# Shared-head queries rotated with their weight alone, the root applied to the row maximum and in the exponential

## The reference, cut to what matters

```
q_g   = axial_rope(rms_norm(heads(gq, 8), q_norm_w))      # norm per token and head, then rotation
k_g   = axial_rope(rms_norm(heads(gk, 2), k_norm_w))
k_all = concat([k_g, rms_norm(ctx keys, k_norm_w)])       # 512 keys
s     = q_g @ k_all^T * 64**-0.5
o     = softmax(s) @ v_all
rms_norm(x, w) = x * rsqrt(mean(x*x) + 1e-6) * w
```

## Time and profile before

| what | value |
| --- | --- |
| median of three runs | 1973.33 us |
| span of the profiled execution | 1967.2 us |
| what lies around the span (median less span) | 6.1 us |
| TensorE busy | 1947.9 us (99%) |
| VectorE busy | 1213.1 us (62%) |
| ScalarE busy | 897.8 us (46%) |
| GpSimd busy | 219.2 us (11%) |
| mean granted TensorE clock | 0.998 |

### The profile page before, as it was taken

How to read it: one execution, slowest core, us unless ns; L and a number is a source line. 1 busy time by engine, 2 the same in 40 slices (tenths; PEclk the granted TensorE clock), 3 DMA queues, 4 the chain that set the end, 5 groups by cost and what they waited for, 6 DMA issues and landing times. The chain is left out here.

```text
span 1967.2 us, 34620 instructions
## 1 busy us (share of the span) xinstructions
PE 1947.9 (99%) x12862; PEld 1699.5 (86%) x12862; DVE 1213.1 (62%) x1950; ACT 897.8 (46%) x1435; POOL 219.2 (11%) x230
## 2 busy tenths in 40 slices
PE   9999999999999999999999999999999999999998
PEld 6777887777787788998998999999998999999997
DVE  6554543355443655546566677896767767677675
ACT  5544322344332544435554445764445444655444
POOL 1000100111122001201101000000001000201000
PEclk9999999999999999999999999999999999999999
DMA  8212444311234322343355555455555555445553
GB/s 331 83 67 75 146 140 135 133 65 57 81 104 156 110 94 97 111 144 112 129 172 182 181 185 179 150 172 185 188 182 193 184 189 182 161 156 184 185 182 118
DMA packets 79426, 289.18 MB, mean 147 GB/s; under 512 B 8912, under 2 KB 9168, under 8 KB 79312
## 3 DMA queue, kind: packets, MB, share of 16 engines
q1 hardware_dynamic: 77760, 282.13, 42.6%
q0 software_dynamic: 1120, 4.72, 0.8%
q10 hardware_dynamic: 432, 0.72, 0.1%
HBM read 286.49 MB, written 1.05 MB: 146 GB/s over the span
## 5 line engine op out<-in xcount | busy, mean ns | idle before, releaser
L1990 DVE TENSOR_TENSOR w_lo<-raw,w_hi 128x1024 fp32r<-128x1024 f32 x484 | 597.4, 1240 | 301.5 <-ACT w_hi L1677 300.1
L1677 ACT ACTIVATE w_hi<-raw 128x1024 fp32r<-128x1024 f32 x484 | 507.1, 1054 | 392.3 <-PE bank L2634 236.7
L2640 PE MATMUL bank<-h,w_hi 128*128 128x512 f32 x1376 | 491.0, 399 | 1.0 <-DVE h L2148 0.7
L2632 PE MATMUL bank<-h,w_hi 128*128 128x512 f32 (+1 forms) x1344 | 474.2, 353 | 1.9 <-DVE h L2202 0.8
L2633 PE MATMUL bank<-h,w_hi 128*128 128x512 f32 (+1 forms) x1344 | 453.0, 337 | 0.0
L2634 PE MATMUL bank<-h,w_lo 128*128 128x512 f32 (+1 forms) x1344 | 452.4, 337 | 0.0
L2642 PE MATMUL bank<-h,w_lo 128*128 128x256 f32 x1376 | 386.2, 281 | 0.0
L2640 PEld LDWEIGHTS bank<-h,w_hi 128*128 128x128 f32 x1376 | 258.7, 188 | 61.7 <-DVE h L2148 1.4
L2632 PEld LDWEIGHTS bank<-h,w_hi 128*128 128x128 f32 x1344 | 254.5, 189 | 56.4 <-issue 29.7
L2634 PEld LDWEIGHTS bank<-h,w_lo 128*128 128x128 f32 x1344 | 254.6, 189 | 28.0
L2633 PEld LDWEIGHTS bank<-h,w_hi 128*128 128x128 f32 x1344 | 255.2, 190 | 21.9
(11 more groups left out here) (261 smaller groups left out, 2361.8 us busy)
## 6 DMA issues: line engine op xcount, KB each, us to landing
raw<-in_weights SPq DMA_DIRECT2D x516, 512.0 KB, 3.3
early<-in_first SPq DMA_DIRECT2D x10, 512.0 KB, 13.4
bias<-in_rpb POOLq DMA_DIRECT2D x8, 384.0 KB, 3.4
early_o<-in_first SPq DMA_DIRECT2D x4, 512.0 KB, 16.7
x<-in_tokens SPq DMA_DIRECT2D x3, 512.0 KB, 7.0
work<-in_first SPq DMA_DIRECT2D x2, 512.0 KB, 16.1
out<-cols_out SPq DMA_DIRECT2D x4, 256.0 KB, 2.9
con<-in_consts SPq DMA_DIRECT2D x1, 544.0 KB, 17.9
```

Of the source, the lines that this page charges most:

```text
L1677: nc.scalar.activation(w_hi[:, n % SPLIT, :], raw[:, t % RAW, :], ACT.Copy).then_inc(hi_ready, 1)
L1990: dve.tensor_tensor(w_lo[:, t % RAW, :], raw[:, t % RAW, :], w_hi[:, SPLIT_NO[t] % SPLIT, :].bitcast(F32), ALU.subtract).then_inc(lo_ready, 1)
L2632: nc.tensor.matmul(dst, w_hi[:, SPLIT_NO[t] % SPLIT, at], hi, start=start, stop=False, skip_group_check=shared)
L2640: nc.tensor.matmul(bank[:, :], w_hi[:, SPLIT_NO[t] % SPLIT, at], h[:, k, 0:BOTH], start=k == 0, stop=k == KC - 1, skip_group_check=True)
```

## The change

Queries lose `head_spread`. ScalarE evacuates a query with its weight as scale into `head_out`, and `rotate` comes one part after `head_norm`, for TensorE and GpSimd behind that copy. GpSimd writes the root per token and head to a table of its own, `q_rstd`. In the softmax of this branch VectorE multiplies each row maximum by the root of its row (two multiplications of 128x1 per unit, behind both maxima), and the exponential takes the root as its scale. Keys are unchanged.

The diff, cut to its core (the wait of `rotate` is changed in TensorE's step as it is in GpSimd's, shown here):

```diff
         def norm():
             st = s.add("head_norm", job=job, what=what, g=g, cols=n, m=s.use("M"), evac=evac,
                        rows=s.count("rows"))
-            s.later(3 if layer and what == "query" and g.c < 2 else 2, lambda: spread(st))
+            if what == "query":
+                g.q_norm = st
+                s.later(1, lambda: rotate(st))
+            else:
+                s.later(2, lambda: spread(st))
...
+        q_rstd = hb("q_rstd", [P, 2, 8])
...
             def rotate_step(st):
-                pool.wait_ge(m_free, st.norm.spread.m + 1)
+                if st.what == "key":
+                    pool.wait_ge(m_free, st.norm.spread.m + 1)
+                else:
+                    pool.wait_ge(head_copied, st.norm.n + 1)
...
             def head_norm_step(st):
-                row_rstd_of(st.m, 2 * st.cols // P)
+                n = 2 * st.cols // P
+                row_rstd_of(st.m, n, q_rstd[:, st.g.slot, 0:n] if st.what == "query" else None)
...
                     use, i = u.s_use + hp, stat(u, hp)
-                    nc.scalar.activation(probs[:, hp, 0:u.keys], S[use % 2][:, 0:u.keys], ACT.Exp,
+                    root = q_rstd[:, u.g.slot, 2 * u.b + hp:2 * u.b + hp + 1] if u.g.branch == "gqa" else 1.0
+                    nc.scalar.activation(probs[:, hp, 0:u.keys], S[use % 2][:, 0:u.keys], ACT.Exp, scale=root,
                                          bias=row_stat[:, 0, i:i + 1], accum_out=row_stat[:, 1, i:i + 1])\
                         .then_inc(s_free[use % 2], 1)
...
-                nc.scalar.activation(head_rows[:, st.n % 2, 0:n], G[st.job.n % 2][:, 0:n], ACT.Copy)\
-                    .then_inc(head_copied, 1)
+                if st.what == "key":
+                    nc.scalar.activation(head_rows[:, st.n % 2, 0:n], G[st.job.n % 2][:, 0:n], ACT.Copy)\
+                        .then_inc(head_copied, 1)
+                else:
+                    act.wait_ge(set_up_dve, 6)
+                    nc.scalar.activation(head_out[:, st.n % 2, 0:n], G[st.job.n % 2][:, 0:n], ACT.Copy,
+                                         scale=q_norm[:, st.g.layer:st.g.layer + 1]).then_inc(head_copied, 1)
...
                     dve.tensor_reduce(row_stat[:, 0, i:i + 1], s[:, 0:u.keys], AX_X, ALU.max, negate=True)\
+                        .then_inc(raw_max if u.g.branch == "gqa" else max_ready, 1)
+                if u.g.branch != "gqa":
+                    return
+                dve.wait_ge(rstd_rows, u.g.q_norm.rows + 1)
+                for hp in range(2):
+                    i = stat(u, hp)
+                    raw_count[0] += 1
+                    dve.wait_ge(raw_max, raw_count[0])
+                    dve.tensor_scalar(row_stat[:, 0, i:i + 1], row_stat[:, 0, i:i + 1],
+                                      q_rstd[:, u.g.slot, 2 * u.b + hp:2 * u.b + hp + 1], None, ALU.mult)\
                         .then_inc(max_ready, 1)
```

More of the change, by code:

```diff
@@ L276, in __init__ @@
         self.key_at, self.keys, self.layer, self.live = key_at, keys, layer, live
+        self.q_norm = None
         self.m, self.m_n, self.mixer, self.norm = m, m_n, mixer, norm
@@ L1322, in block_kernel @@
         max_ready = sem("max_ready")
+        raw_max = sem("raw_max")
         sum_ready = sem("sum_ready")
@@ L1573, in merge_step, with row_rstd_of @@
                 pool.tensor_tensor(v, v, branch_sum[:, st.dc % 2, 0:st.cols], ALU.add).then_inc(added, 1)
-            def row_rstd_of(m, n):
+            def row_rstd_of(m, n, dst=None):
                 pool.wait_ge(m_free, m + 1)
-                pool.tensor_tensor(row_rstd[:, 0:n], row_mean[:, 0:n], neg_half[:, 0:1].to_broadcast([P, n]), ALU.pow)\
+                pool.tensor_tensor(row_rstd[:, 0:n] if dst is None else dst, row_mean[:, 0:n], neg_half[:, 0:1].to_broadcast([P, n]), ALU.pow)\
                     .then_inc(rstd_rows, 1)
@@ L2290, in scores_step @@
                     dve.tensor_reduce(row_stat[:, 0, i:i + 1], s[:, 0:u.keys], AX_X, ALU.max, negate=True)\
+                        .then_inc(raw_max if u.g.branch == "gqa" else max_ready, 1)
[8 more added lines that the diff above has]
+                                      q_rstd[:, u.g.slot, 2 * u.b + hp:2 * u.b + hp + 1], None, ALU.mult)\
                         .then_inc(max_ready, 1)
+            raw_count = [0]
             def scale_probs_step(st):
@@ L2373, in head_spread_step @@
                 at = PARAM_AT["k_norm_w"] + st.g.layer
-                w = par[:, at:at + 1] if st.what == "key" else q_norm[:, st.g.layer:st.g.layer + 1]
+                w = par[:, at:at + 1]
                 dve.wait_ge(m_full, st.m + 1)
@@ L2934, in rotate_step @@
             def rotate_step(st):
-                pe.wait_ge(m_free, st.norm.spread.m + 1)
+                if st.what == "key":
+                    pe.wait_ge(m_free, st.norm.spread.m + 1)
+                else:
+                    pe.wait_ge(head_copied, st.norm.n + 1)
                 pe.wait_ge(m_free, st.m)
```

## The result

In the runs that compare the two kernels, nine of each, the changed kernel took 1979.05 us in the median (1976.72 to 1981.39) and the kernel before 1974.56 (1971.35 to 1977.24). The ratio is 1.0024, with a 95% interval from 1.0016 to 1.0033: slower by 4.5 us (3.2 to 6.5). The forecast was 4.1 us slower, and 1977.4 us.

A forecast was written before the change was run, and what follows sets the result against it. TensorE was taken to set the time (busy 1947.9 of 1967.2 us). Layer 0's -3.05 and layer 1's +7.15 (2.65 + 2.6 + 1.9) gave +4.1 us on the 1973.33 median: 1977.4 us, range 1974.5 to 1980.5.

The forecast's parts named there:

- The sum: Whole program: layer 0 -3.05 and layer 1 +7.15 us, together +4.1 us, 1977.4 us; chance 0.55.
- TensorE sets the time, and a spread taken from it is gained: Spread of 8 queries on TensorE: removing it saves 4.1 us in layer 0 and 2.35 in layer 1, 6.45 together.
- The exponential behind both maxima and a multiplication: Softmax: exponential starts 0.7 us later with 512 keys, multiplication taken at 0.16; a unit's probabilities come 0.87 us later.
- Layer 1, query 0: Moved rotation: 0.4 us lost for the mean and 2.0 for the gate's bank, 0.78 saved; TensorE 1.7 us late.
- Layer 1, query 1: Rotation ahead of query 0's turn copies: values start 2.55 us late, about 2.65 with the second unit.
- Layer 1, queries 2 and 3: Copies behind rotation and split: 1.3 us lost, 0.15 for the swap, 0.49 saved; about 0.95 net each, 1.9.
- Layer 0: Bank behind query 0 costs 0.5 us, query 1's turn 0.5, queries 2 and 3 gain 0.93 each; gain 3.05 us.
- (a): Rival: TensorE loses 6.45 us of work and nothing waits, the gate behind layer 1's query 0 deciding: 1966.9 us; chance 0.08.
- (b): Rival: waits half as large, layer 1's first units keeping some cover, some 3 us go: 1974.4 us; chance 0.22.
- (c): Rival: multiplications stop 0.4 us each, powers locked out at 2.55; seven layer 1 places cost 0.5 more each: 1981.5; chance 0.15.
- (d): Rival: nothing on the path, spread hidden behind other work and softmax has room; counted within the chance of (b).
- The rule on the shared ports: Layer 1, queries 2 and 3: cosine begun within a VectorE split ends about 0.7 us behind it, sum unchanged.

The follow-up runs named there:

- e9: Changed kernel with the rotation back in its old slot and the root left out of the softmax: stretches 668.57 us, -5.85 against the kernel before.
- e10: Changed kernel, rotation still early, with the root left out of the softmax: stretches 673.88 us, -0.54 against the kernel before.
- e5: Changed kernel with only query 0's rotation back in its old slot, in both layers: stretches 676.06 us, +1.64 against the kernel before.
- e7: Kernel before, with one more part of a product between first scores and turn in layer 1: median 1978.88 us, ratio 1.0024.
- e1: Changed kernel with the rotation back at about its old place: stretches 672.92 us, -1.50 against the kernel before; median 1974.13 us, ratio 1.0004.
- e4: Kernel before plus the softmax part alone (two multiplications and the exponential's scale, by ones): stretches 678.83 us, +4.41 against the kernel before.
- e3: Changed kernel with the rotation in its old slot and each maximum multiplied at once: median 1971.72 us, ratio 0.9984 to the kernel before.
- e8: Changed kernel, maxima multiplied at once, one more product part before layer 1's turns, only layer 1 query 1 rotated early: stretches 672.49 us, -1.93 against before.

## Why the prediction was right

**The sum.** +4.00 us by the stretches for +4.1, and the time inside its range. The mechanism held step by step, as told below, but that the total came within 0.1 us is partly luck: layer 0 gained 0.31 us less than forecast and layer 1 lost 0.41 less, and the two cancel. The 1979.05 us lie 1.65 above the forecast's 1977.4; 1.23 of them are the kernel before, which has 1974.56 here and had 1973.33 then.

**TensorE sets the time, and a spread taken from it is gained.** Right. Layer 0 gains 4.14 us when nothing waits (e9), against 4.1. Layer 1 gives 1.71 us of 2.35 in e9: TensorE comes to its turns sooner and waits 0.6 us at two of them (0.2 in the kernel before), even with the old softmax. Most of what is missing is at the turn of query 0, between its first and second scores: of the 0.59 us of query 1's spread, which stood there, 0.14 is gained.

**The exponential behind both maxima and a multiplication.** Right in form, a little low in size. The multiplication was taken at 0.16 us, the row of the reciprocal. It took 0.204 us. The tile's view of the kernel after, duration in ns (min/median/max) and first and last start:

```profile
L2316 DVE TENSOR_SCALAR row_stat<-row_stat,q_rstd x48: 196/204/213, 397.5 to 974.0; 128x1 f32<-128x1 f32 x48
L1800 ACT ACTIVATE work<-bank,row_stat,q_rstd x48: 552/769/782, 397.7 to 974.9; 128x512 f32<-128x512 f32 x32, 128x256 f32<-128x256 f32 x16
L1800 ACT ACTIVATE work<-bank,row_stat x48: 465/679/691, 65.3 to 756.7; 128x512 f32<-128x512 f32 x32, 128x256 f32<-128x256 f32 x16
```

The second and third line are the same instruction with two operands per row and with one, in the two branches of one kernel: 0.090 us apart in the median, as worked out from two rows of 384 columns. The probabilities came 0.92 us later, 0.87 forecast; the three turns between a query's two scores cost 0.90, 0.91 and 0.91.

**Layer 1, query 0.** Right: 0.47 us for the mean (0.4) and 1.71 for the gate's bank (2.0), and the first scores come 1.69 us late (1.7). The two waits less the 0.78 of the spread would be only 1.40: TensorE came to the bank 0.4 us later than reckoned (893.10, which is 890.23 on the clock of the earlier trace rows, 2.87 us earlier, for 889.8). That made the wait shorter and changed nothing else, since it is the gate that says when TensorE goes on, and the gate ended at 894.66, which is 891.79 on that clock, for 891.75. The timeline of VectorE shows the chain step by step: swap's product, sum behind the cosine, remainder behind ScalarE's rounding, split, gate.

```profile
890.26 0.42 DVE L2414 TENSOR_TENSOR scaled<-bank,con 128x256 f32<-128x256 f32 x1 [0.85 <-PE bank L2970]
891.25 0.43 DVE L2417 TENSOR_TENSOR head_out<-head_rows,scaled 128x256 f32<-128x256 f32 x1 [0.56 <-POOL head_rows L1574]
892.22 0.43 DVE L2421 TENSOR_TENSOR q_s<-head_out,q_s 128x256 fp32r<-128x256 f32 x1 [0.55 <-ACT q_s L1761]
893.10 1.23 DVE L2007 TENSOR_TENSOR w_lo<-raw,w_hi 128x1024 fp32r<-128x1024 f32 x1 [0.45 <-ACT w_hi L1688]
894.25 0.41 DVE L2243 SCALAR_TENSOR_TENSOR branch_gate<-scaled,bank 128x256 f32<-128x256 f32 x1
```

**Layer 1, query 1.** The term that was most off. The values start 2.51 us late (2.55), and the steps ahead of them (scaling, split, sum, rounding, copies) lie within 0.1 us of the chain in the forecast. But I added 0.1 for the second unit. Instead 0.25 came back: the second values start 2.26 us late, because the wait of 0.5 us that stood there before was gone. TensorE came so late to the second unit that the copies were ready. A wait that exists already is slack for a delay of TensorE ahead of it, and the sum should have taken it off. It accounts for most of the 0.41 us by which layer 1 came out under its 7.15: 0.1 added, 0.25 not taken off.

**Layer 1, queries 2 and 3.** Right: the values waited 1.23 and 1.24 us (1.3); net 0.89 and 0.86 (0.95).

**Layer 0.** 0.51 for the bank (0.5), 0.41 for the turn (0.5); -2.74 for -3.05. The waits were right (but the turn's needs the early place and the later softmax together, where the forecast held that layer 0 covers the softmax's delay), and the gain came out 0.3 lower: queries 0 and 1 together kept 1.0 us of 1.2, queries 2 and 3 0.90 and 0.88 of 0.93 each. The experiments say where: of the 4.14 us of e9 the place takes 0.66 (e10), where its wait is 0.51, and the softmax beside it 0.74, where its wait is 0.41. A stop cost 0.15 to 0.33 us more than its idle time; why stays open.

**The rivals.** (a), all waits covered, is what e9 comes near to, and needs both the old place and a free softmax; the bank behind query 0, named as the place that decides, is the dearest single place (2.4 us by e5), though without it the change would still lose 1.6. (b), waits half as large, falls by the table of starts: no step was below nine tenths of its size but query 1's. (c), dearer waits, falls too: the multiplication took no stop of 0.4 us (1.45 us from the maxima to the exponential against 1.41), and the power of query 0 in layer 0 took 1.64 us, not 2.55, as the split had left that place. (d), that the spread was hidden, falls by e9.

**The rule on the shared ports.** The forecast put the cosine product of query 2 within a split and said that it would end about 0.7 us behind it, when the sine is done, and change nothing. The timeline of GpSimd:

```profile
927.99 1.02 POOL L1588 TENSOR_TENSOR q_rstd<-stats,neg_half 128x4 f32<-128x4 f32 x1 [11.01 <-DVE stats L2150]
928.99 0.90 POOL L1574 TENSOR_TENSOR head_rows<-head_out,con 128x256 f32<-128x256 f32 x1
```

VectorE's split ran from 928.06 to 929.29, so the cosine ended 0.60 us behind it. That it was held up agrees with the Trainium skill ("SBUF — State Buffer", section "SBUF: two separate sides"), by which whichever of the two starts first has the shared ports for its whole instruction. So does the power in e7, which began 0.14 us into a split and took 1.94 us where 1.01 is its time alone. In both the operation ended a little sooner than its whole time alone behind the split's end: 0.60 us for 0.74, and 0.85 for 1.01. By the same rule the split that began 0.07 us behind the power above should have been held up, and it wasn't: its 1.23 us are those of any other. There the measurement decides.

## What to carry to other kernels

Work that a chain of small steps hands from one engine to the next has a place in every queue it passes: when it moves, price each thing behind it in each queue, not only the instruction that was saved. Here a move of two or three parts cost 5.3 us and a 0.9 us longer softmax 4.5, against 5.85 us gained by leaving out 96 matmuls; with the place undone, the two small steps paired and one more part of cover, the same idea is worth 0.27%. A wait that is already there absorbs a delay of the engine that waits (query 1 above), but not one of the work that it waits for: in e1 and e4, where TensorE was less late, the same wait grew from 0.5 us to 1.3 and 1.5. And extra cover at one place lengthens the queue for another (e7).

## What was not expected of the hardware

A multiplication of 128x1 by a per-row scalar takes 0.204 us, more than a reciprocal of the same shape (0.164), and in the paired order (e3) an idle 0.11 us stands between the first maximum and the multiplication that waits for it (0.04 at the second), so that even this order delays the exponential by 0.33 us (1.04 for 0.71).

The power of 4 columns that began 0.07 us *ahead* of a split (927.99 and 928.06 above) took its usual 1.02 us, and the split its usual 1.23, though they overlap for 0.95 us. The same is so at other distances, in the kernel before: a power of 4 columns that began 0.57 us ahead of a split (921.45) took 1.02 us and the split 1.23, one of 2 columns 0.10 us ahead (1717.60) 0.70 and 1.21. The powers and cosines that were stretched had begun within a split. Why the two run beside each other when GpSimd is first stays open.

A stop of 3.4 us of TensorE was followed by a granted clock of 0.50 (e8), which cost some 2.3 us on top; behind the stop of 2.87 us in e7 the clock stayed at 1.00.
